# Both feed-forward projections of a two-layer decoder as block products with seven products in place of eight, on one Trainium2 core

## The chip, the core and the metric

One core of a Trainium2 chip runs the whole program in one launch. The metric is the device time of one execution in microseconds. Five engines work side by side, each through its own list of instructions in order: TensorE (PE, with its weight loads as PEld), VectorE (DVE), ScalarE (ACT), GpSimd (POOL) and SyncE (SP, which issues the DMAs). They meet only at semaphores that the kernel sets and waits for by hand.

## What is computed

The reference is one step of a hybrid decoder with two layers over 1024 prompt tokens and 8 sample tokens, all in float32: token mixer, cross attention, and the feed-forward part, which is what changes here.

```python
def conv_ffn(h, w_up_l, conv_w_l, conv_b_l, w_down_l, buf):
    u = h @ w_up_l                                   # 1032 tokens x 1024 @ 1024 x 5632
    L = u.shape[1]
    up = jnp.concatenate([buf.astype(u.dtype), u], axis=1)
    c = conv_b_l
    for j in range(CONV_W):                          # causal, depthwise, width 3
        c = c + up[:, j:j + L] * conv_w_l[j]
    a, b = jnp.split(c, 2, axis=-1)
    y = (jax.nn.silu(a) * b) @ w_down_l              # 2816 x 1024
    return y, up[:, -(CONV_W - 1):]
```

Before it h is an RMSNorm of x, and behind it x += RMSNorm(y).

## The kernel before

Everything is kept with features on the 128 partitions and the T = 1032 tokens along the free axis; `xT`, `hh`, `hl`, `Y` are tiles of 8 feature blocks by 1032 tokens. A float32 product is made of three TensorE products of the type float32r: each operand is split into a high part and the rest (`hh` and `hl` of the input, `w_hi` and `w_lo` of a weight), and `mm3` (L260) issues high by high, high by low and low by high into one PSUM bank, each with its own 128x128 weight load. ScalarE writes the high part as a copy into float32r, and a subtraction gives the low part.

Weights come as slabs of 128x1024 in an order fixed at build time (`weight_plan`, L87): SP loads one into `w_raw` (2 buffers, L230), ScalarE writes `w_hi` (3 slots, L239), GpSimd `w_lo` (L247). The plan keeps the three a few slabs ahead of TensorE.

The feed-forward part is in `stage_cross_ffn` (L1790). Its hidden features are 22 blocks j, each with two halves a and b. For a block, `up(j, 0)` and `up(j, 1)` (L2307) make the two halves of u: for each of three chunks of 344 tokens 8 feature blocks by `mm3`, so 24 matmuls into a bank, 144 for both. VectorE scales them out of PSUM into `f_u` (L2619), ScalarE starts the convolution (L2457), VectorE adds the two earlier taps (L2627 for the prompt, L2629 for the 8 samples), ScalarE applies silu (L2462), VectorE multiplies the halves (L2635), and the gate result is split in two (`f_ghi` L2473, `f_glo` L2639). `down(j)` (L2290) multiplies it at once by the rows of w_down that belong to block j: 8 output blocks by 3 chunks by 3 matmuls, 72 in all, and VectorE adds each of the 24 results into `Y` (L2654). `down(j - 1)` stands behind `up(j, 1)` on TensorE, so a block's convolution has the time of other matmuls to finish. One layer has 22 x 144 + 22 x 72 = 4752 of these matmuls, all of 344 columns.

The first block is made by `first_up` (L2192), between the last products of the cross attention's output (units of 264 columns) and the sums of squares for the norms. The last two blocks' down part, chunk by chunk, is in the class `End` (L1891 on), together with the post-norm, the residual and, after layer 0, the pre-norm of the next layer's mixer (`stage_mixer`); after layer 1 `stage_last` (L2708) does it.

## Time and profile before

| what | us |
| --- | --- |
| runs (3), median | 3277.84 (3276.75 to 3281.5) |
| profiled execution, span from its first to its last instruction | 3276.6 |
| PE busy in it | 3187.7 |
| DVE busy | 2197.5 |
| ACT busy | 1194.9 |
| POOL busy | 674.7 |
| feed-forward stretch without a pause on PE, layer 0 | 900 to 1592 |
| the same, layer 1 | 2528 to 3221 |

For the profiled execution only the span is on hand; the median of the runs lies 1.2 us above it. Matmuls overlap in their pipeline, so a matmul's own duration is longer than the distance from one start to the next; it is that distance that counts. The idle time beside a group is the engine's wait ahead of it, with what ended most of it.

### The profile page before, as it was taken

To read this page: it belongs to the slowest core of one execution; us is meant where nothing else is said; L and a number is where in the kernel's file an instruction comes from. 1 tells how busy PE (TensorE), PEld (TensorE's weight loads), DVE (VectorE), ACT (ScalarE), POOL (GpSimd) and SP (SyncE) were. 2 spreads that over 40 slices of the span, in tenths; PEclk is the share of its full clock that TensorE was granted. 3 is DMA by queue.
4 is the path that set the end of the run, shared out by engine and by line. 5 is a ranking of instruction groups with operands and counts; after the bars stand their busy time and mean duration, and the time that the engine had idled before them with its cause. 6 is when DMAs were issued, how large, how long until landed. Compare 5 with 4: busy or idle time off the path is not lost. (4 is left out here: it accounts for less than half of the span.)

```text
span 3276.6 us, 51631 instructions
## 1 busy us (share of the span) xinstructions
PE 3187.7 (97%) x21768; PEld 3034.5 (93%) x21768; DVE 2197.5 (67%) x3283; ACT 1194.9 (36%) x1904; POOL 674.7 (21%) x270
## 2 busy tenths in 40 slices
PE   8999999999999999999999999999999999999998
PEld 8999789988899999999989997899878999999997
DVE  7877764554577777777777877544545777767776
ACT  6443554344422212222445425543434122221214
POOL 1111241112321222212111113302113222122220
PEclk9999999999999999999999999999999999999999
DMA  5112342216211111111121123422152111111111
GB/s 187 47 47 66 93 147 98 78 51 232 70 46 46 47 51 40 52 46 52 51 87 41 53 65 95 173 73 78 52 225 69 52 42 51 44 52 46 46 52 60
DMA packets 80486, 245.85 MB, mean 75 GB/s; under 512 B 8064, under 2 KB 32896, under 8 KB 76672
## 3 DMA queue, kind: packets, MB, share of 16 engines
q1 hardware_dynamic: 79968, 242.50, 21.4%
q8 instruction: 172, 2.82, 0.3%
q14 instruction: 58, 0.48, 0.0%
q10 hardware_dynamic: 288, 0.06, 0.0%
HBM read 214.20 MB, written 23.04 MB: 72 GB/s over the span
## 5 line engine op out<-in xcount | busy, mean ns | idle before, releaser
L262 PE MATMUL ps<-hh,w_hi 128*128 128x344 f32 (+2 forms) x4320 | 1408.5, 326 | 30.1 <-DVE hl L1132 9.9
L264 PE MATMUL ps<-hh,w_lo 128*128 128x344 f32 (+2 forms) x4320 | 1383.0, 320 | 0.0
L263 PE MATMUL ps<-hl,w_hi 128*128 128x344 f32 (+2 forms) x4320 | 1382.8, 320 | 0.0
L247 POOL TENSOR_TENSOR w_lo<-w_raw,w_hi 128x1024 fp32r<-128x1024 f32 x266 | 674.5, 2538 | 2547.3 <-ACT w_hi L239 2547.3
L262 PEld LDWEIGHTS ps<-hh,w_hi 128*128 128x128 f32 x4320 | 815.0, 189 | 53.2 <-issue 22.2
L263 PEld LDWEIGHTS ps<-hl,w_hi 128*128 128x128 f32 x4320 | 814.9, 189 | 3.0 <-issue 0.2
L264 PEld LDWEIGHTS ps<-hh,w_lo 128*128 128x128 f32 x4320 | 814.9, 189 | 0.0
L2654 DVE TENSOR_TENSOR Y<-Y,ps 128x344 f32<-128x344 f32 x912 | 432.6, 513 | 155.7 <-PE ps L264 155.7
L239 ACT ACTIVATE w_hi<-w_raw 128x1024 fp32r<-128x1024 f32 x296 | 311.4, 1054 | 427.1 <-PE ps L264 379.9
L2457 ACT ACTIVATE f_c<-f_u,cT 128x1032 f32<-128x1032 f32 (+1 forms) x92 | 111.4, 1212 | 633.9 <-DVE f_u L2619 627.1
L263 PE MATMUL ps<-f_glo,w_hi 128*128 128x344 f32 x960 | 307.3, 320 | 0.0
L264 PE MATMUL ps<-f_ghi,w_lo 128*128 128x344 f32 x960 | 307.2, 320 | 0.0
L262 PE MATMUL ps<-f_ghi,w_hi 128*128 128x344 f32 x960 | 306.6, 319 | 0.0
L2627 DVE SCALAR_TENSOR_TENSOR f_c<-f_u,cT,f_c 128x1024 f32<-128x1024 f32 x172 | 225.2, 1309 | 98.6 <-ACT f_c L2457 95.6
L262 PEld LDWEIGHTS ps<-f_ghi,w_hi 128*128 128x128 f32 x960 | 181.1, 189 | 0.0
L264 PEld LDWEIGHTS ps<-f_ghi,w_lo 128*128 128x128 f32 x960 | 180.4, 188 | 0.0
L263 PEld LDWEIGHTS ps<-f_glo,w_hi 128*128 128x128 f32 x960 | 180.2, 188 | 0.0
L2619 DVE TENSOR_TENSOR f_u<-ps,rs 128x1032 f32<-128x1032 f32 x86 | 105.7, 1229 | 66.9 <-PE ps L264 66.7
L2629 DVE SCALAR_TENSOR_TENSOR f_c<-f_cache,cT,f_c 128x8 f32<-128x8 f32 x172 | 124.0, 721 | 6.2
L2473 ACT ACTIVATE f_ghi<-f_c 128x1032 fp32r<-128x1032 f32 x42 | 44.8, 1067 | 149.7 <-DVE f_c L2635 149.7
L1161 DVE TENSOR_TENSOR Y<-ps,rs 128x344 f32<-128x344 f32 x120 | 59.7, 508 | 47.1 <-PE ps L264 37.0
L1648 DVE TENSOR_TENSOR oq_acc<-oq_acc,oq_sq 128x384 f32<-128x384 f32 (+1 forms) x54 | 27.8, 516 | 93.3 <-ACT oq_sq L1571 91.4
(352 smaller groups left out, 3600.5 us busy)
## 6 DMA issues: line engine op xcount, KB each, us to landing
w_raw<-in_w_stream SPq DMA_DIRECT2D x296, 512.0 KB, 3.4
out_y_cols<-xT SPq DMA_DIRECT2D x6, 1376.0 KB, 8.1
xT<-out_y_cols SPq DMA_DIRECT2D x2, 4128.0 KB, 13.0
mem_keys<-in_cache_mem_k SPq DMA_DIRECT2D x6, 1024.0 KB, 5.1
Y<-in_cache_mem_k SPq DMA_DIRECT2D x6, 1024.0 KB, 7.4
mem_values<-in_cache_mem_v SPq DMA_DIRECT2D x6, 1024.0 KB, 7.9
mem_keys<-in_cache_mem_v SPq DMA_DIRECT2D x6, 1024.0 KB, 7.8
hg_set<-Y SPq DMA_DIRECT2D x32, 129.0 KB, 2.3
```

What stands on the lines that cost most here:

```text
L239: nc.scalar.activation(w_hi[:, SLOT[m], :], w_raw[:, m % RR, :], ACT.Copy).then_inc(hi_done, 1)
L247: nc.gpsimd.tensor_tensor(w_lo[:, SLOT[m], :], w_raw[:, m % RR, :], w_hi[:, SLOT[m], :].bitcast(F32), ALU.subtract).then_inc(lo_done["pool ...
L262: nc.tensor.matmul(out, whi, mhi, start=start, stop=False)
L263: nc.tensor.matmul(out, whi, mlo, start=False, stop=False)
L264: return nc.tensor.matmul(out, wlo, mhi, start=False, stop=stop)
L1161: nc.vector.tensor_tensor(dst[:, cols(c)], ps[:, u % 3, 0:CH], rs[:, cols(c)], ALU.mult)\
L2457: nc.scalar.activation(C[:, h, at], U[:, h, 2 + at.start:2 + at.stop], ACT.Identity, bias=cT[:, l, 3, col:col + 1], scale=cT[:, l, 2, col: ...
L2473: nc.scalar.activation(gh[:, j % 2, :], C[:, 1, :], ACT.Copy).then_inc(f_gh, 1)
L2619: nc.vector.tensor_tensor(tokens3(U[:, h, 2:2 + T]), ps[:, 3 * h:3 * h + 3, 0:CH], tokens3(rs[:]), ALU.mult).then_inc(f_up, 1)
L2627: dve_c(nc.vector.scalar_tensor_tensor(c[:, 0:SEQ], U[:, h, t:t + SEQ], w, c[:, 0:SEQ], ALU.mult, ALU.add))
L2629: dve_c(nc.vector.scalar_tensor_tensor(c[:, SEQ:T], ca[:, col, t, :], w, c[:, SEQ:T], ALU.mult, ALU.add))
L2654: nc.vector.tensor_tensor(y, y, b, ALU.add).then_inc(f_y, 1)
```

## The change

It treats both projections as two-by-two block products and forms each by seven products instead of eight (Winograd's form). The program of the feed-forward part is now 34 units per layer: 22 for the up-projection (a unit makes block j of both halves a and b) and 12 for the down-projection (three groups over the hidden features of 8, 8 and 6 blocks; in each 4 pairs of output blocks). Of the two-by-two split, the contracted features are cut in halves of 4 blocks (3 in the last group), the outputs are the unit's two blocks, and the tokens are cut into `cols4` quarters of 258: a pair of quarters is one two-by-two column split, and p = A or B says which pair. So a unit is 7 products x 2 pairs, each of 4 `mm3` (3 in the last group) on 258 columns: 168 matmuls (126), 5544 per layer.

What is new around them:

- The products' operands are sums and differences of blocks. For a unit's weights VectorE makes four of them, 128x512 each (`combine_block`, L2906); ScalarE writes the high part of all seven (`high_block`, L2615) and GpSimd the low part (`low_block`, L2252). Six half slots form the ring, so a block can be written when the product six blocks earlier is done.
- For the moving side there are seven operands per pair: of the normed input, once per layer, and of the gate results, at the start of each down group. VectorE makes four per pair (`combine`, L2875), and the high part is ScalarE's (14 copies); the low part is made in place, 10 by VectorE (`low`, L2897) and 4 by GpSimd (`low`, L2264).
- A product's PSUM bank stays open and later products add to it; each state is read out once. Of the 14 read-outs of a unit, VectorE adds 6 (`add_out`, L2923) and ScalarE copies 8 (`copy_out`); from unit 26 on VectorE does all 14.
- The gate result goes to DRAM (`gates`) and comes back by group in 8 loads of 4 (3) blocks by 258 columns. x is spilled to the output in DRAM and comes back at the layer's end; the result of the down part builds up in `xT`.
- The convolution adds both earlier taps of the samples in one 128x8 addition.
- The up-projection's scaling by the norm moves from PSUM to the input (`operand_of_x`).

The diff, cut to its core:

```diff
+QT = T // 4
+P_11, P_T1, P_T2, P_22, P_T3, P_21, P_T4 = range(NP)
+LANDS = [(0, 0), (1, 1), (0, 1), (0, 1), (1, 1), (0, 0), (1, 0)]
...
+def steps_of(n):
+    if n:
+        return [(n, c, p) for c in range(NP) for p in range(2)]
+    return [(0, c, p) for p in range(2) for c in range(NP - 1)] + [(0, NP - 1, p) for p in range(2)]
+def read_by(n, c):
+    return "act" if c in FIRST_TOUCH and n < FT + F_PAIRS else "dve"
...
+                def step(n, c, p):
+                        if n not in (0, *STARTS) or p == A:
+                            pe.wait_ge(f_wlo, NP * n + c + 1)
+                        if n in STARTS:
+                            low_ready(pe, STARTS.index(n), c, p)
+                        if c == P_11:
+                            if n >= 2:
+                                wait_read(pe, n - 2, P_T4, p)
...
+                            wait_read(pe, n, {P_T2: P_11, P_22: P_T1, P_T3: P_T2, P_T4: P_T3}[c], p)
...
+                        for k in range(nk):
+                            w = slice(P * k, P * k + P)
+                            last = mm3(ps[:, bank_of(n, c, p), 0:QT], block(w_hi, n, c)[:, w], block(w_lo, n, c)[:, w], high[:, k, :],
+                                       low[:, k, :], fresh and k == 0, k == nk - 1, c != P_21)
...
+                    def combine(g, c, p):
+                        if c == P_T1:
+                            x, y = plain(P_T1, p, nk), plain(P_11, p, nk)
+                        elif c == P_T2:
+                            x, y = plain(P_22, p, nk), plain(P_T1, p, nk)
+                        elif c == P_T3:
+                            x, y = plain(P_T2, p, nk), plain(P_11, p, nk)
+                        else:
+                            x, y = source_21(g, p, nk), plain(P_T2, p, nk)
...
+                        nc.vector.tensor_tensor(plain(c, p, nk), x, y, ALU.subtract).then_inc(f_t, 1)
+                    def low(g, c, p):
+                        dve.wait_ge(f_chi, hi_no(g, c, p))
+                        dve.wait_ge(f_t, t_no(g, READ_OF[c], p))
...
+                    for n in range(1, N_UNITS):
+                        if here:
+                            for p in (A, B):
+                                combine(here, P_T4, p)
+                            for c, p in ((P_T2, A), (P_T2, B), (P_T3, A), (P_21, A), (P_T4, A)):
+                                low(here, c, p)
+                        if n <= FT:
+                            conv(n - 1, 0)
+                        add_out(n, P_11, A)
+                        add_out(n, P_11, B)
+                        if n <= FT:
+                            conv(n - 1, 1)
+                            gate(n - 1)
...
+                        if n < LAST:
+                            combine_block(n + 1, P_T1)
+                        if after:
+                            for p in (A, B):
+                                combine(after, P_T1, p)
+                        add_out(n, P_22, A)
+                        add_out(n, P_22, B)
+                        if n < LAST:
+                            combine_block(n + 1, P_T2)
+                        add_out(n, P_T3, A)
+                        add_out(n, P_T3, B)
+                        if n < LAST:
+                            combine_block(n + 1, P_22)
+                        if after:
+                            for c in (P_T2, P_T3):
+                                for p in (A, B):
+                                    combine(after, c, p)
+                        add_out(n, P_21, A)
+                        add_out(n, P_21, B)
+                        if n < LAST:
+                            combine_block(n + 1, P_T3)
+                        if after:
+                            for c, p in ((P_T1, A), (P_T1, B), (P_11, A), (P_11, B), (P_22, A)):
+                                low(after, c, p)
...
-                    for j in range(1, FT):
-                        up(j, 0)
-                        up(j, 1)
-                        if j < FT - 1:
-                            down(j - 1)
+                    for n in range(1, N_UNITS):
+                        for c in range(NP):
+                            for p in (A, B):
+                                step(n, c, p)
```

VectorE's list in the middle of the feed-forward part of layer 0, one block j before (`f_u` is u, `f_c` the convolution, `Y` the down result):

```order
L2619 TENSOR_TENSOR f_u<-ps,rs 128x1032
L2622 COPY f_tail<-f_u 128x10
L2627 SCALAR_TENSOR_TENSOR f_c<-f_u,cT,f_c 128x1024
L2629 SCALAR_TENSOR_TENSOR f_c<-f_cache,cT,f_c 128x8
L2654 TENSOR_TENSOR Y<-Y,ps 128x344 x24
L2635 TENSOR_TENSOR f_c<-f_c 128x1032
L2639 TENSOR_TENSOR f_glo<-f_c,f_ghi 128x1032
```

and the same engine and place of the changed kernel, one up unit:

```order
L2952 SCALAR_TENSOR_TENSOR f_c<-f_u,cT,f_c 128x1024
L2954 TENSOR_TENSOR f_c<-f_c,f_cache 128x8
L2956 SCALAR_TENSOR_TENSOR f_c<-f_u,cT,f_c 128x1024
L2962 TENSOR_TENSOR f_c<-f_c 128x1032
L2921 TENSOR_TENSOR w_lo_f<-w_raw 128x512
L2932 TENSOR_TENSOR f_u<-f_u,ps 128x258 x2
L2921 TENSOR_TENSOR w_lo_f<-w_lo_f,w_raw 128x512
L2921 TENSOR_TENSOR w_lo_f<-w_raw,w_lo_f 128x512
```

The scaling and the 24 additions out of PSUM are gone from it; the four weight combinations (L2921) stand between six additions of 258 columns (L2932).

VectorE's list at the start of the second down group, from unit 25 into unit 26 (`hl_f` and `f_t_f` are `hl` and the tile of the last operand read as float32):

```order
L2895 TENSOR_TENSOR hl_f<-hl_f 128x4x258 x2
L2932 TENSOR_TENSOR xT<-xT,ps 128x258 x2
L2921 TENSOR_TENSOR w_lo_f<-w_lo_f,w_raw 128x512
L2895 TENSOR_TENSOR Y<-hl_f 128x4x258 x2
L2903 TENSOR_TENSOR hl<-hl_f,hh 128x4x258 x5
L2895 TENSOR_TENSOR f_t_f<-f_u,hl_f 128x4x258 x2
L2903 TENSOR_TENSOR hl<-hl_f,hh 128x4x258 x2
L2903 TENSOR_TENSOR Y_r<-Y,Y_r 128x4x258
L2903 TENSOR_TENSOR Y_r<-f_u,Y_r 128x4x258
L2903 TENSOR_TENSOR f_t<-f_t_f,f_t 128x4x258
L2932 TENSOR_TENSOR xT<-xT,ps 128x258 x6
```

Here 18 operations of 1032 columns stand in one run of the list, ahead of unit 26's first six read-outs. GpSimd's list at the same place:

```order
L2262 TENSOR_TENSOR w_lo<-w_lo_f,w_hi 128x512 x4
L2270 TENSOR_TENSOR hl<-hl_f,hh 128x4x258
L2262 TENSOR_TENSOR w_lo<-w_raw,w_hi 128x512
L2270 TENSOR_TENSOR Y_r<-Y,Y_r 128x4x258
L2270 TENSOR_TENSOR Y_r<-f_u,Y_r 128x4x258
L2270 TENSOR_TENSOR f_t<-f_t_f,f_t 128x4x258
```

Before, GpSimd had three subtractions of 128x1024 per block j; now it has seven of 128x512 per unit, and four of 1032 columns at each group's start.

## Rows read from the trace of the kernel before

**Rows 1.** The page: span and engines' busy time.

```profile
span 3276.6 us, 51631 instructions
...
PE 3187.7 (97%) x21768; PEld 3034.5 (93%) x21768; DVE 2197.5 (67%) x3283; ACT 1194.9 (36%) x1904; POOL 674.7 (21%) x270
```

**Rows 2.** Busy time by stretch: feed-forward part of layer 0, steady.

```profile
core 0: us, PE busy (x) PEld busy (x) DVE busy (x) ACT busy (x) POOL busy (x), PEclk, DMA share, GB/s
900.00:1592.00 692.00, 692.00 (x4398) 692.00 (x4397) 501.26 (x772) 156.62 (x147) 150.34 (x61) 1.00 0.14 46
```

**Rows 3.** Timeline, PE: matmuls of 256 and 264 columns; columns: start us, us.

```profile
367.11 0.28 PE L264 MATMUL ps<-mem_hi,w_lo 128*128 128x256 f32 x1
...
367.46 0.28 PE L264 MATMUL ps<-mem_hi,w_lo 128*128 128x256 f32 x1
...
829.74 0.28 PE L262 MATMUL ps<-hh,w_hi 128*128 128x264 f32 x1
...
835.91 0.29 PE L262 MATMUL ps<-hh,w_hi 128*128 128x264 f32 x1
```

**Rows 4.** Groups by shape, DVE: name, shapes, count, busy us, mean ns, idle before.

```profile
L2627 DVE SCALAR_TENSOR_TENSOR f_c<-f_u,cT,f_c 128x1024 f32<-128x1024 f32 x172 | 225.2, 1309 | 98.6 <-ACT f_c L2457 95.6
...
L2635 DVE TENSOR_TENSOR f_c<-f_c 128x1032 f32<-128x1032 f32 x42 | 51.8, 1234 | 6.5 <-DVE f_c L2629 0.5
...
L1199 DVE TENSOR_TENSOR hg_work<-hg_work,xT 128x512 f32<-128x512 f32 x20 | 13.9, 693 | 0.7
...
L653 DVE TENSOR_TENSOR mem_keys<-ps,mrs 128x256 f32<-128x256 f32 x32 | 13.4, 420 | 23.0 <-PE ps L264 22.8
```

**Rows 5.** One line, POOL's subtraction: duration ns min/median/max.

```profile
L247 POOL TENSOR_TENSOR w_lo<-w_raw,w_hi x266: 2354/2412/5464, 17.0 to 3219.8; 128x1024 fp32r<-128x1024 f32 x133
```

**Rows 6.** Additions out of PSUM, one line, DVE: duration ns min/median/max.

```profile
L2654 DVE TENSOR_TENSOR Y<-Y,ps x912: 511/514/515, 947.2 to 3199.1; 128x344 f32<-128x344 f32 x183
```

**Rows 7.** Timeline, POOL against DVE, feed-forward and before it.

```profile
1006.92 2.56 POOL L247 TENSOR_TENSOR w_lo<-w_raw,w_hi 128x1024 fp32r<-128x1024 f32 x1 [2.77 <-ACT w_hi L239]
...
1007.25 2.25 DVE L2629 SCALAR_TENSOR_TENSOR f_c<-f_cache,cT,f_c 128x8 f32<-128x8 f32 x1
...
1010.86 0.23 DVE L2629 SCALAR_TENSOR_TENSOR f_c<-f_cache,cT,f_c 128x8 f32<-128x8 f32 x1
...
834.28 12.48 POOL L247 TENSOR_TENSOR w_lo<-w_raw,w_hi 128x1024 fp32r<-128x1024 f32 x3 [1.15 <-ACT w_hi L239]
...
836.38 5.43 DVE L2541 TENSOR_TENSOR xT<-xT,Y 128x3072 f32<-128x3072 f32 x1
```

**Rows 8.** Groups by shape, ACT.

```profile
L2347 ACT ACTIVATE x_probsT<-ps 128x512 f32<-128x512 f32 x32 | 19.1, 597 | 31.2 <-PE ps L2141 31.2
```

**Rows 9.** DMA issues: KB each, median us to landing.

```profile
w_raw<-in_w_stream SPq DMA_DIRECT2D x296, 512.0 KB, 3.4
...
xT<-in_mem_cols SPq DMA_DIRECT2D x4, 512.0 KB, 5.5
```

**Rows 10.** Busy time by stretch: the first block of layer 0.

```profile
856.90:888.90 32.00, 30.88 (x173) 27.89 (x172) 11.04 (x14) 14.32 (x33) 3.68 (x2) 1.00 0.15 54
```

**Rows 11.** End of layer 0's feed-forward: first matmul of End, last evacuation read.

```profile
L1926 PE MATMUL ps<-f_ghi,w_hi x96: 314/320/626, 1592.5 to 3259.4; 128*128 128x344 f32 x96
...
1683.44 0.52 DVE L1161 TENSOR_TENSOR Y<-ps,rs 128x344 f32<-128x344 f32 x1 [3.25 <-PE ps L264]
```

**Rows 12.** The norm at a layer's end, and the last operation.

```profile
L2032 DVE TENSOR_TENSOR Y<-Y,rs 128x2752 f32<-128x2752 f32 x3 | 9.1, 3019 | 0.0
...
L2053 DVE SCALAR_TENSOR_TENSOR xT<-Y,gT,xT 128x344 f32<-128x344 f32 x24 | 12.0, 568 | 0.0
...
3271.23 1.59 DVE L2048 TENSOR_TENSOR xT<-xT,Y 128x1376 f32<-128x1376 f32 x1
```

**Rows 13.** Timeline, PE, after a pause of 2.53 us.

```profile
3227.32 0.63 PE L1926 MATMUL ps<-f_ghi,w_hi 128*128 128x344 f32 x1 [2.53 <-DVE f_glo L2688]
...
3230.72 0.32 PE L1926 MATMUL ps<-f_ghi,w_hi 128*128 128x344 f32 x1
```

1134 lines of the change are left out of this document (667 added, 467 removed).

## Prediction

> **What bounds the kernel now.** I read the page first: PE is busy for 3187.7 of 3276.6 us, DVE for 67%, ACT and POOL for 36% and 21% [rows 1]. Then the busy time by stretch: in layer 0's feed-forward part PE does not pause at all for 692 us; 4398 matmuls in 692 us are one per 0.1573 us [rows 2]. So TensorE's matmuls set the time there, and everything else hides behind them. A change that takes matmuls away can gain, as long as what it hands to DVE, POOL and ACT still hides. Last I read how DVE and POOL get on with each other, since the change loads these two.
>
> **Matmuls removed.** Before: 2 x 4752 = 9504 of 344 columns x 0.1573 = 1495 us. Now 2 x 5544 = 11088 of 258 columns. The nearest shapes are 256 columns, three starts in 0.35 us = 0.117 each, and 264 columns, 51 starts in 6.17 us = 0.121 [rows 3]. I take 0.118, since 258 is nearest to 256: 1308 us. That is **-187 us** (0.117: -198; 0.121: -153). It needs no weight load to come late: the rows at 256 columns load a 128x128 weight per matmul too and keep 0.117. For the fixed part of a matmul the Trainium skill ("TensorE: Matmul & The Clock Gate", the section "Wait — 56ns, not 53.3ns?") gives columns by 2.4 GHz plus 2.5 ns; by it the two sums would be 1386 and 1220 us and the gain 166. The trace has 14 ns over the columns' time at 344 and 10 to 11 at 256 and 264, so I keep the rows' sum.
>
> **The other engines in an up unit.** A unit gives PE 168 x 0.118 = 19.8 us. VectorE's list in it: four taps at 1.31, the product of the halves 1.23, four weight combinations like the 128x512 rows at 0.69 [rows 4], two operations on the samples at 0.23 [rows 7], six additions out of PSUM like the 256-column row at 0.42 [rows 4], 0.35 for two small copies: 12.6 us. GpSimd: seven subtractions of half the width of a row with median 2.41 [rows 5], 1.2 each, 8.4 us. Each alone fits. But they exclude each other: POOL's subtraction ran from 1006.92 to 1009.48, and DVE's 128x8 operation, 0.23 us on its own, started at 1007.25 and took 2.25, until that end. The other way round, DVE's 5.43 us from 836.38 made three POOL subtractions take 12.48 in place of 7.2 [rows 7]. The 912 additions with one operand in PSUM show no such delay: none took over 515 ns [rows 6]. The Trainium skill says it too ("GPSIMD Engine Reference", section "1. Specifications"): GpSimd's SBUF interfaces are shared with VectorE, with contention for instructions with two SBUF inputs. Without the exclusion VectorE would have 7 us to spare per unit; with it, 12.6 + 8.4 = 21.0, less about 1.9 of POOL's work that falls beside PSUM additions or a pause, plus some 20 handovers of 0.05 (an estimate; POOL's end at 1009.48 and DVE's at 1009.50 are of that size), is 20.2. T4's step needs T3's read-out with only three steps (4.2 us) between, so PE soon follows VectorE: 0.4 x 21 units x 2 layers = **+17 us** (0 if it all fits, +84 at 21.8 per unit, with nothing of POOL's beside anything).
>
> **Starts of the down groups.** At unit 22, 26 and 30 fourteen operands must be made while the old ones are still read. The order is forced: T3's operand is T2's minus 11's, and the low part of 11 overwrites 11, so the first step of the group waits for the combinations T1, T2, T3 and then the low part of 11. Time 0 is the start of the unit ahead. The gate loads (0.5 MB each, like the mem_cols rows of 5.5 us when issued in pairs) go out as steps 11 and T1 free their tiles, and the next weights behind them, 3.4 us each alone [rows 9]; I put the second half at 13. From there VectorE does four weight combinations 2.8, six combinations of 1032 columns at 1.23 = 7.4, six additions 2.5, three low parts 3.7: 16.4 us; POOL's four weight parts and one low part of 1032 (2.4) cost 7.2 more, 1.7 of it beside additions. ACT's high parts (0.6 for 512 columns [rows 8], about twice that for 1032) stay ahead of that. So the first step starts at 35 where it was due at 19.8: 15 us. Behind it, in unit 26, nine operations of 1032 and one addition (11.5) with POOL's 9.6 stand ahead of the read-out of 11 that T2's step needs, against 5.7 us of PE work: 15 more. Group 1 reaches much the same sum by another way: 7 us at T2 and 7 at T4, since VectorE first has the last block's taps and product. Group 3 has three blocks for four: 24. Sum 84 per layer, **+168 us**. Without the exclusion the same list gives 14, 15 and 11, +80 in all; the top is some 95 per layer, +190, if the gate loads land 4 us later.
>
> **Start of the feed-forward part.** Before, PE was busy for 30.88 of the 32.0 us of the first block [rows 10]. Now unit 0 waits for operands that VectorE and GpSimd make one after the other: for pair A 16 scalings, 4 combinations and the low parts, with the last norm and residual of the cross attention in the middle of VectorE's list and the weight combinations 22 and T3 behind these; for pair B all again once the last mean is known. With the prices above, step 22 A starts some 10 us late, T3 and 21 2 us each, 11 B 11 us, T1 B and T2 B some 4 each. That is 34 per layer, **+68 us** (27 per layer without the exclusion, 42 as the top: +54 to +84).
>
> **Ends of the layers.** From the first matmul of the last two blocks at 1592.5 to the ninth unit of the next mixer at 1683.4 [rows 11], 91 us hold 360 matmuls of 0.157 = 57 of real work, so 34 of sums and waits. Now 24 sums become 3 of three matmuls, but norm (3.02), residual (8 x 0.57 [rows 12]), tree and low parts of each chunk start only behind the last read-out, in a row on VectorE; my chain for the same nine units has 34 us beside the matmuls too. At the end of layer 1: read-out, squares, sum and root 4.1, six halves of 1.59 + 4 x 0.51, and the last store 3.8 (before, the last operation ended at 3272.8, 3.8 before the end [rows 12]): 30, about what sums, waits and the last chunk's norm take there now. **0 us**, between -6 and +15.
>
> **The clock.** After a pause of 2.53 us the next 12 matmuls took the 3.40 us to 3230.72, near the rate of 1.2 GHz and not of 2.4, which cost 1.5 us [rows 13]. The starts above make some ten longer pauses per layer, but half of the slow matmuls run ahead of a further wait: **+10 us** (5 to 30).
>
> **Sum.** 3276.6 - 187 + 17 + 168 + 68 + 0 + 10 = 3352.6; the median of the runs lies 1.2 above the profiled span: **3353 us**, slower.
>
> **The rivals.**
> 1. Faster. The operations of GpSimd fall into VectorE's pauses and delay nobody. Then only the chains of dependence are left: 3278 - 187 + 0 + 80 + 54 - 3 + 5 = 3227 us. For it: VectorE's list has room in the light down units. Against it: at the group starts its list is dense just where GpSimd has most to do, and every row of an overlap shows full exclusion. It decides at 93 us of loss per layer: below it the change gains.
> 2. Slower still. The up units run at 21.8, all of VectorE's and GpSimd's work in a row: 67 more, 3420 us. Against it: POOL's first subtraction of a unit waits for the weights, when VectorE waits too.
> 3. The change does not do what it says: weight loads cannot keep pace at 258 columns, say 0.140 per matmul, +244 us, about 3597. The 0.117 at 256 columns speaks against it.
>
> **How the numbers follow.** A measurement of this kernel tells 0.2% (6.5 us) from no change. Chances: the forecast 0.63 (3300 to 3400, by its own bounds), rival 1 0.17, rival 2 0.15, rival 3 0.02, within 0.2% by chance of the terms 0.03. Range: down to 3240, which takes in most of rival 1, and up to 3430 for rival 2. Faster 0.17, same 0.03, slower 0.80.
>
> **What would show it.** In the changed kernel's profile: matmuls of 258 columns starting 0.118 apart (0.14 would show rival 3); up units of 20.2 us (19.8 or 21.8 for the rivals), with subtractions of POOL stretched beyond 1.2 us and taps beyond 1.3; PE idle of about 15 us ahead of the first step of units 22, 26, 30, released by VectorE's low part, and a second wait in the same unit; some 30 us of PE idle in unit 0; GpSimd busy about 45% of the feed-forward stretch. If PE's waits there add up to less than 93 us per layer, the sign of the forecast is wrong.

## The result, and the profile after

The changed kernel takes 3350.4 us (median of 4 runs, 3348.6 to 3351.2) against 3278.2 us (4 runs, 3276.8 to 3281.5): the ratio is 1.022, 95% interval 1.0206 to 1.0235. It is slower by 72 us. The profiled execution has a span of 3349.3 us against 3276.6 before, so the two traces differ by 72.7 us, and that is what follows accounts for.

First the page of the changed kernel, to be held against [rows 1]. TensorE is busy 134 us less in a span that is 73 us longer; GpSimd is busy 1.7 times as long.

```profile
span 3349.3 us, 57862 instructions
...
PE 3053.3 (91%) x23292; PEld 2903.8 (87%) x23292; DVE 2233.6 (67%) x3027; ACT 1498.5 (45%) x2616; POOL 1177.3 (35%) x664
```

Next the busy time by stretch, layer 0's feed-forward part: unit 0 with the work around it, the steady up units, then by turns the start of a down group and the calm units behind it. The columns are: stretch (start and end in us) and its length, then busy us (and instructions) of PE, PEld, DVE, ACT and POOL, the granted clock, DMA share and GB/s.

```profile
856.00:940.00 84.00, 56.17 (x372) 53.14 (x372) 57.71 (x69) 36.48 (x64) 41.61 (x23) 0.82 0.26 88
940.00:1345.00 405.00, 405.00 (x3378) 405.00 (x3378) 316.24 (x383) 208.86 (x364) 214.23 (x140) 1.00 0.26 88
1345.00:1400.00 55.00, 33.02 (x210) 31.71 (x210) 49.65 (x45) 26.09 (x38) 31.71 (x16) 0.75 0.15 50
1400.00:1457.00 57.00, 56.02 (x467) 55.82 (x466) 14.70 (x25) 21.44 (x43) 21.27 (x17) 1.00 0.40 128
1457.00:1510.00 53.00, 27.39 (x190) 27.05 (x191) 44.84 (x41) 17.34 (x23) 30.58 (x15) 0.74 0.07 23
1510.00:1568.00 58.00, 58.00 (x485) 57.90 (x483) 23.70 (x49) 14.34 (x22) 22.65 (x18) 1.00 0.34 106
1568.00:1625.00 57.00, 37.63 (x268) 37.19 (x268) 43.49 (x60) 18.07 (x28) 29.65 (x21) 0.82 0.10 28
```

Where [rows 2] showed one stretch without a pause, there are now two kinds. In the up units and the calm down units PE never pauses, and VectorE has room (316 of 405 us). In unit 0 and at the three group starts VectorE is busy 69% to 90% of the time, PE 52% to 67%, and the granted clock falls to 0.74 to 0.82.

What the steady stretch gives: 405.00 us by 3378 matmuls is 0.1199 us each, 20.1 us per unit, with PE busy throughout. 11088 x 0.1199 = 1329 us, so the matmuls gained **166 us**.

What the rest takes back shows in PE's timeline (start, us, engine, line, operation, operands; in brackets the idle time before it and its releaser, where "issue" means that the profile shows none). These are the longest waits of unit 0 and all of group 2's start; the second of the latter is step 11 A of unit 26, which needs VectorE's low part.

```profile
881.88 0.55 PE L325 MATMUL ps<-hh,w_hi 128*128 128x258 f32 x1 [9.12 <-ACT f_u L2648]
...
907.96 0.58 PE L325 MATMUL ps<-hh,w_hi 128*128 128x258 f32 x1 [13.06 <-DVE hl L2903]
...
1458.25 0.36 PE L325 MATMUL ps<-f_t,w_hi 128*128 128x258 f32 x1 [2.22 <-DVE xT L2932]
...
1474.53 0.55 PE L325 MATMUL ps<-hh,w_hi 128*128 128x258 f32 x1 [13.15 <-issue]
...
1494.42 0.55 PE L325 MATMUL ps<-hh,w_hi 128*128 128x258 f32 x1 [11.21 <-DVE xT L2932]
```

Added up over such rows, PE's waits in layer 0 are 27.5 us in unit 0 and 21.8, 26.6 and 19.4 us at the group starts; in layer 1 they are 28.0, 21.1, 27.7 and 18.3. That is **190 us** (waits of 0.3 us and more). Beside them PE was busy longer for its matmuls in these stretches: 33.02 us for 210 of them is 7.8 more than at 0.12 each, and the other three stretches give 4.6, 5.5 and 11.5, 29 per layer, **59 us**. Some 38 us of these are matmuls at the lower clock: 212 in layer 0 and 186 in layer 1 start 0.215 apart in place of 0.1199; the rest is mostly the ends of the last matmuls ahead of waits and, in unit 0, products of another kind. The distances agree: the 5544 matmuls of a layer take 790.3 and 787.9 us from the first to the last, 249 us more than 0.1199 each. The ends of the layers gave back some 7: from the last matmul at 1656.5 to the ninth unit's read-out at 1720.7 there are 64 us, of which 30 beside matmuls (34 before), and at the end of layer 1 there are 29.8 us (32 before). In all -166 + 190 + 59 - 7 = +76, where 72.7 was measured.

VectorE's timeline says what those waits are for. This is the start of group 2: unit 25 begins at 1438.6, unit 26 is due at 1459.

```profile
1453.05 1.16 DVE L2921 TENSOR_TENSOR w_lo_f<-w_raw 128x512 f32<-128x512 f32 x1 [15.78 <-DMA w_raw<-in_w_stream]
1454.14 2.36 DVE L2895 TENSOR_TENSOR hl_f<-hl_f 128x1032 f32<-128x1032 f32 x2
...
1459.67 3.45 DVE L2895 TENSOR_TENSOR hl_f<-hl_f 128x1032 f32<-128x1032 f32 x2
1463.04 3.45 DVE L2895 TENSOR_TENSOR Y<-hl_f 128x1032 f32<-128x1032 f32 x2
...
1467.68 11.94 DVE L2903 TENSOR_TENSOR hl<-hl_f,hh 128x1032 fp32r<-128x1032 f32 x5
1479.54 2.37 DVE L2895 TENSOR_TENSOR f_t_f<-f_u,hl_f 128x1032 f32<-128x1032 f32 x2
1481.83 5.45 DVE L2903 TENSOR_TENSOR hl<-hl_f,hh 128x1032 fp32r<-128x1032 f32 x2
1487.20 3.38 DVE L2903 TENSOR_TENSOR Y_r<-Y,Y_r 128x1032 fp32r<-128x1032 f32 x1
...
1493.86 1.41 DVE L2932 TENSOR_TENSOR xT<-xT,ps 128x258 f32<-128x258 f32 x4
```

From the landing of the weights to the four additions VectorE has no pause. Step 11 A starts inside the five low parts, at 1474.53, when the third of them, its own, has just ended (1474.42); T2 A needs the first of the four additions and starts at 1494.42. The five low parts take 2.4 us each in the mean, where one takes 1.22 when nothing disturbs it. The next rows show why. First one line's durations over the whole run (ns, min/median/max), for an operation of 8 columns, the low parts of 1032, GpSimd's subtraction and the additions out of PSUM; then both timelines in a steady up unit.

```profile
L2954 DVE TENSOR_TENSOR f_c<-f_c,f_cache x88: 151/1254/1273, 933.4 to 3051.0; 128x8 f32<-128x8 f32 x88
L2903 DVE TENSOR_TENSOR hl<-hl_f,hh x54: 951/2024/3421, 864.9 to 3252.8; 128x1032 fp32r<-128x1032 f32 x40, 128x774 fp32r<-128x774 f32 x14
L2262 POOL TENSOR_TENSOR w_lo<-w_lo_f,w_hi x272: 1011/1296/2268, 869.7 to 3304.1; 128x512 fp32r<-128x512 f32 x120, 128x384 fp32r<-128x384 f32 x16
L2932 DVE TENSOR_TENSOR xT<-xT,ps x404: 406/423/426, 940.1 to 3319.5; 128x258 f32<-128x258 f32 x135
```

```profile
1005.80 1.27 DVE L2954 TENSOR_TENSOR f_c<-f_c,f_cache 128x8 f32<-128x8 f32 x1
...
1008.18 1.26 DVE L2951 COPY f_tail<-f_u 128x10 f32<-128x10 f32 x1
```

```profile
1005.09 1.95 POOL L2262 TENSOR_TENSOR w_lo<-w_lo_f,w_hi 128x512 fp32r<-128x512 f32 x1 [1.48 <-ACT w_hi L2625]
```

GpSimd's subtraction started at 1005.09 and ended at 1007.04; the operation of 8 columns, 0.15 us on its own, started at 1005.80 and ended at 1007.07. As in [rows 7], the two engines take turns by whole instructions, and an addition with one operand in PSUM (at most 426 ns in 404) is held by nobody, as in [rows 6].

### The profile page after: what moved, and what is told of

Same layout as the page of the kernel before. It is cut to its first block and busy times, and to the rows that moved or that the text cites. A ratio compares the mean times of both kernels' runs of the same rounds, so it can differ in the third digit from the quotient of the medians.

```text
span 3349.3 us, 57862 instructions
## 1 busy us (share of the span) xinstructions
PE 3053.3 (91%) x23292; PEld 2903.8 (87%) x23292; DVE 2233.6 (67%) x3027; ACT 1498.5 (45%) x2616; POOL 1177.3 (35%) x664
## 3 DMA queue, kind: packets, MB, share of 16 engines
q1 hardware_dynamic: 122752, 305.91, 27.4%
## 5 line engine op out<-in xcount | busy, mean ns | idle before, releaser
L325 PE MATMUL ps<-hh,w_hi 128*128 128x258 f32 (+3 forms) x4320 | 1352.0, 313 | 199.7 <-issue 73.2
L326 PE MATMUL ps<-hl,w_hi 128*128 128x258 f32 (+3 forms) x4320 | 1322.0, 306 | 0.0
L327 PE MATMUL ps<-hh,w_lo 128*128 128x258 f32 (+3 forms) x4320 | 1320.8, 306 | 0.0
L310 POOL TENSOR_TENSOR w_lo<-w_raw,w_hi 128x1024 fp32r<-128x1024 f32 x134 | 349.8, 2614 | 1365.0 <-ACT w_hi L302 1365.0
L2262 POOL TENSOR_TENSOR w_lo<-w_lo_f,w_hi 128x512 fp32r<-128x512 f32 (+1 forms) x272 | 380.1, 1410 | 403.6 <-DVE w_lo_f L2921 301.9
L2262 POOL TENSOR_TENSOR w_lo<-w_raw,w_hi 128x512 fp32r<-128x512 f32 (+1 forms) x204 | 319.4, 1567 | 339.3 <-ACT w_hi L2625 336.2
L325 PE MATMUL ps<-Y_r,w_hi 128*128 128x258 f32 x1056 | 301.1, 285 | 16.4 <-ACT xT L2648 14.1
L326 PE MATMUL ps<-Y_r,w_hi 128*128 128x258 f32 x1056 | 302.0, 286 | 0.0
L2932 DVE TENSOR_TENSOR xT<-xT,ps 128x258 f32<-128x258 f32 x404 | 164.8, 419 | 203.7 <-PE ps L327 203.3
L327 PE MATMUL ps<-Y_r,w_lo 128*128 128x258 f32 x1056 | 299.3, 283 | 0.0
L2921 DVE TENSOR_TENSOR w_lo_f<-w_raw 128x512 f32<-128x512 f32 (+1 forms) x136 | 141.8, 1042 | 143.6 <-DMA w_raw<-in_w_stream 121.9
L325 PEld LDWEIGHTS ps<-Y_r,w_hi 128*128 128x128 f32 x1056 | 200.9, 190 | 18.1 <-issue 14.8
L327 PEld LDWEIGHTS ps<-Y_r,w_lo 128*128 128x128 f32 x1056 | 203.3, 192 | 0.0
L326 PEld LDWEIGHTS ps<-Y_r,w_hi 128*128 128x128 f32 x1056 | 201.7, 191 | 0.0
```

The lines of the kernel that those rows point to most:

```text
L310: nc.gpsimd.tensor_tensor(w_lo[:, SLOT[m], :], w_raw[:, m % RR, :], w_hi[:, SLOT[m], :].bitcast(F32), ALU.subtract).then_inc(lo_done["pool ...
L325: nc.tensor.matmul(out, whi, mhi, start=start, stop=False, skip_group_check=reopened)
L326: nc.tensor.matmul(out, whi, mlo, start=False, stop=False, skip_group_check=reopened)
L327: return nc.tensor.matmul(out, wlo, mhi, start=False, stop=stop, skip_group_check=reopened)
L2262: nc.gpsimd.tensor_tensor(to, whole_block, block(w_hi, n, c).bitcast(F32), ALU.subtract).then_inc(f_wlo, 1)
L2921: nc.vector.tensor_tensor(block(w_lo_f, n, c), x, y, op).then_inc(f_wadd, 1)
```

## The experiments

The rows above leave two readings: the starts are long because GpSimd and VectorE hold each other out, or because of the orders and loads in them (late weights, low parts ahead of read-outs). A third question is what the slow clock adds. No run leaves out all of the operand work of the starts, so its whole price stays open.

All times are medians against runs of the kernel before on the same chip; it stayed within 3276.9 and 3278.6 us. For reading them, PE's waits in layer 0 by place, in us, added up from the timelines (waits of 0.7 us and more):

| kernel | time, us | unit 0 | group 1 | group 2 | group 3 | sum |
|---|---|---|---|---|---|---|
| the change | 3350.4 | 27.5 | 21.4 | 26.6 | 19.4 | 95 |
| e1_pool_fill | 3246.7 | 23.7 | 11.7 | 10.8 | 7.0 | 53 |
| e2_readout_first | 3326.9 | 27.4 | 21.2 | 19.5 | 12.0 | 80 |
| e3_low11_first | 3350.4 | 27.4 | 21.7 | 24.6 | 17.4 | 91 |
| e4_start_order | 3351.4 | 25.6 | 21.1 | 26.4 | 19.4 | 93 |
| e6_raw_first | 3358.5 | 27.4 | 26.4 | 26.6 | 18.4 | 99 |
| e7_hold_pool | 3331.8 | 27.7 | 24.9 | 19.9 | 14.8 | 87 |
| e9_vector_weights | 3315.5 | 26.6 | 22.1 | 18.7 | 13.1 | 81 |
| e11_late_conv | 3300.3 | 26.7 | 15.8 | 16.1 | 12.4 | 71 |
| e12_all | 3296.9 | 25.6 | 18.0 | 17.0 | 9.8 | 70 |

**e1: GpSimd writes without reading.**

```diff
-    nc.gpsimd.tensor_tensor(to, whole_block, block(w_hi, n, c).bitcast(F32), ALU.subtract).then_inc(f_wlo, 1)
+    nc.gpsimd.memset(to.bitcast(F32), 0.0).then_inc(f_wlo, 1)
...
-    nc.gpsimd.tensor_tensor(operand(c, 1, p, nk), x, operand(c, 0, p, nk).bitcast(F32), ALU.subtract)
+    nc.gpsimd.memset(operand(c, 1, p, nk).bitcast(F32), 0.0).then_inc(f_lop, 1)
```

> GpSimd's low-part subtractions of the feed-forward part (weight blocks, and its four operands of a start) write a constant instead, at the same width: the low parts of all weight blocks and of those operands are left out; VectorE, ScalarE and TensorE issue what they did. It prices how far GpSimd's two-input subtractions stretch VectorE at the starts. Theory (they hold each other out): VectorE's low parts of 1032 columns fall from 2.3-2.4 us to about 1.2, its blocks to 0.69, TensorE's waits at the starts from 190 us to about 100, and the time by 70 to 95 us, to about 3268. Rival (the starts are bound by the late raw weights and by the order of the read-outs, VectorE's own durations matter little): less than 20 us, 3330 or more. If a fill holds VectorE as a subtraction does, the durations do not fall, and the run tells nothing of the two.

Measured: 3246.7 us, 104 below the change and below the kernel before (ratio 0.9909, 0.9894 to 0.9923). VectorE's program is the same, and its lines read (same view as above, one line up in the file):

```profile
L2953 DVE TENSOR_TENSOR f_c<-f_c,f_cache x88: 152/159/167, 921.1 to 2979.9; 128x8 f32<-128x8 f32 x88
...
L2902 DVE TENSOR_TENSOR hl<-hl_f,hh x54: 951/1225/1235, 863.0 to 3157.1; 128x1032 fp32r<-128x1032 f32 x40, 128x774 fp32r<-128x774 f32 x14
...
L2950 DVE COPY f_tail<-f_u x44: 172/173/474, 919.9 to 2936.9; 128x10 f32<-128x10 f32 x44
...
1429.86 0.69 DVE L2920 TENSOR_TENSOR w_lo_f<-w_raw 128x512 f32<-128x512 f32 x1 [15.02 <-DMA w_raw<-in_w_stream]
...
1455.62 1.41 DVE L2931 TENSOR_TENSOR xT<-xT,ps 128x258 f32<-128x258 f32 x4
```

None of these operations is stretched any more: 1254 became 159 ns, 2024 became 1225. PE's waits fall by 42 us in layer 0 and 38 in layer 1, 80 in all; most of the other 24 are matmuls at a higher clock (granted 0.86 or more in each of the seven stretches). The run also takes work away from GpSimd (its blocks come after 0.53 us where they took 1.3 or more), so it prices GpSimd's subtractions as a whole: holding VectorE, and being late themselves. Its two timeline lines part the two at group 2: VectorE's row of the same 28 operations, from the first weight block to the first addition, takes 25.8 us, where it was 40.8 (1453.05 to 1493.86), and that is 15 of the 16 us that this start costs less (the distances of its steps over 0.1199 a matmul went from 31.5 to 15.4). So there nearly all of it is VectorE held out. Over both layers the six group starts cost 83 us where they cost 171, but unit 0 still costs 66 where it was 77: its price is for the most part another (e4). The Trainium skill ("GPSIMD Engine Reference", section "1. Specifications") names contention for VectorE's instructions with two SBUF inputs or in a two-port mode. The trace agrees for the first kind; the copy of 10 columns has one input and was held as well, 1.26 us, and no run shows in which mode it ran.

**e2: the read-outs ahead of the last low parts.**

```diff
-                            for c, p in ((P_T2, A), (P_T2, B), (P_T3, A), (P_21, A), (P_T4, A)):
+                            add_out(n, P_11, A)
+                            add_out(n, P_11, B)
+                            low(here, P_T2, A)
+                            add_out(n, P_T1, A)
+                            add_out(n, P_T1, B)
+                            for c, p in ((P_T2, B), (P_T3, A), (P_21, A), (P_T4, A)):
                                 low(here, c, p)
...
```

> In the first unit of each down group VectorE reads out products 11 and T1 ahead of its last low parts instead of behind them (same work, other order). Theory (TensorE stands 9 to 13 us in that unit because its banks wait behind five low parts): the 11.2, 9.1 and 5.8 us waits released by VectorE's or ScalarE's addition shrink, the low parts of T2, T3, 21 come 1 to 2 us later; in all 10 to 32 us less, about 3326. Rival (the low parts are just as late for the steps that use them, so the wait only changes its name): within 8 us of 3350.

Measured: 3326.9 us, 24 less (ratio to before 1.0151, 1.0134 to 1.0168). PE's timeline at group 2:

```profile
1458.54 0.36 PE L325 MATMUL ps<-f_t,w_hi 128*128 128x258 f32 x1 [1.81 <-DVE xT L2932]
...
1474.83 0.55 PE L325 MATMUL ps<-hh,w_hi 128*128 128x258 f32 x1 [13.16 <-issue]
...
1486.83 0.55 PE L325 MATMUL ps<-hh,w_hi 128*128 128x258 f32 x1 [4.57 <-DVE hl L2903]
```

The wait of 11.2 us became one of 4.6 us, now for the low part itself. From T4's step to T2's it is 28.3 us where it was 36.2. Group 1 did not move (21.2 against 21.4), and that stayed open until e11.

**e3: the low part that TensorE asks for first.**

```diff
-for c, p in ((P_T1, A), (P_T1, B), (P_11, A), (P_11, B), (P_22, A)):
+for c, p in ((P_11, A), (P_11, B), (P_T1, A), (P_T1, B), (P_22, A)):
```

> The low parts of product 11, which is multiplied first, are made ahead of those of T1 at the starts of the three down groups (same work, other order). Theory (TensorE stands at each start for the low part of 11, made third and fourth of a row at 2.4 us each): 13.2, 13.2 and 9.4 us waits shrink by about 4.5 each, six times, 20 to 29 us less, about 3325. Rival (the wait moves to T1, the second product): under 8 us.

Measured: 3350.4 us, no change; the rival held. PE at group 2:

```profile
1455.16 0.36 PE L325 MATMUL ps<-f_t,w_hi 128*128 128x258 f32 x1 [1.00 <-DVE xT L2932]
...
1465.91 0.56 PE L325 MATMUL ps<-hh,w_hi 128*128 128x258 f32 x1 [7.63 <-issue]
...
1491.37 0.55 PE L325 MATMUL ps<-hh,w_hi 128*128 128x258 f32 x1 [15.97 <-DVE xT L2932]
```

Step 11 A does start 5.5 us earlier behind T4's step (10.8 us, not 16.3), and T2 A starts exactly where it did: 36.2 us behind it in both kernels. The 5.5 us moved into the next wait. VectorE's row fixes the end of the stretch, and here the longest wait inside it is worth nothing by itself.

**e4: another order in unit 0.**

```diff
                     low(0, P_T2, A)
-                    normalise(4)
-                    residual(2)
                     combine_block(0, P_22)
                     combine_block(0, P_T3)
+                    normalise(4)
+                    residual(2)
```

> At the start of the feed-forward part VectorE makes the weight combinations 22 and T3 of unit 0 ahead of a normalisation and two residual steps of the output projection instead of behind them (same work, other order). Theory (TensorE's 9.1 us wait, once a layer, is for that chain): it goes, the 13.1 us wait behind it may grow by what is now done later, and the time falls by 10 to 18 us, to about 3336. Rival (the wait only moves to the B pair's operands, which stand behind the moved normalisation): within 5 us of 3350.

Measured: 3351.4 us; the rival held. The wait of 9.1 us became two of 4.3 and 2.6, and step 11 B still waits 13.1 us. In layer 1 it starts 62.2 us behind the matmul of the cross attention's output that waits 2.6 us, before and after the edit. Unit 0 ends with a row of the same kind, that of pair B, which can't start before the last mean.

**e6: raw weights ahead of the gates.**

```diff
                    for n in range(N_UNITS):
                        g = STARTS.index(n + 1) if n + 1 in STARTS else 0
-                        if g:
-                            for q in (P_11, P_T1):
...
                        if n < LAST:
                            load_raw(n + 1, 0)
                            load_raw(n + 1, 1)
...
+                        if g:
+                            for q in (P_11, P_T1):
```

> In the unit ahead of a down group the raw weights of the next unit are loaded ahead of the gates instead of behind the first four gate transfers. Theory (VectorE stands 15.8 us for raw weights and its row of combinations starts that late): the weights land some 5 us earlier, the gates some 3 us later, VectorE's row starts 2 to 4 us earlier in six starts, 12 to 24 us less, about 3332. Rival (the gates are then the last to land and the row waits for them): within 5 us of 3350.

Measured: 3358.5 us, 8 more than the change. The gates of group 2 land at 1457.6, 4.5 us behind the weights, and step 11 A of group 2 follows that of group 1 after 112.8 us, where it was 113.0: nothing gained. At group 1 a new wait came up. ScalarE's timeline, then PE's:

```profile
1341.33 1.06 ACT L2637 ACTIVATE hh<-hl_f 128x1032 fp32r<-128x1032 f32 x1 [7.91 <-DMA hl_f<-gates]
```

```profile
1345.27 0.55 PE L325 MATMUL ps<-Y_r,w_hi 128*128 128x258 f32 x1 [6.50 <-ACT xT L2648]
```

ScalarE's list has the gates' high parts ahead of a silu and two read-outs; it stood 7.9 us for the gates, and TensorE 6.5 us, at step T3 A of unit 21, for the read-outs behind. Neither theory nor rival had named that.

**e7: GpSimd holds back.** On e2:

```diff
                            if n in STARTS:
+                                pool.wait_ge(f_lo, nth(LO_ORDER, LO_LATER, STARTS.index(n), P_T2, A))
                                low(STARTS.index(n), P_T3, B)
```

> On e2_readout_first (3326.9): in the first unit of a down group GpSimd waits with its low part of T3 B until VectorE has made that of T2 A, which TensorE waits for; same work. Theory (GpSimd's subtractions hold VectorE's row out for as long as they run): 4 to 6 us of GpSimd's work leave the row ahead of T2 A, TensorE's wait there (4.6 us at the second group) shrinks by 2 to 4 us in six starts, 12 to 24 us less, about 3310. Rival (GpSimd's parts come too late for steps 21 and T4 and the wait moves there): within 5 us of 3327, or above it.

Measured: 3331.8 us, 5 above e2. The low part of T2 A came earlier (waits of 1.3 and 1.1 us where there were 4.6 and 2.6), and the same time was lost at step T3 A: 11.1 us at group 1, 4.5 and 3.6 at the others. In group 1 the total is again the same:

```profile
1345.97 0.36 PE L325 MATMUL ps<-f_t,w_hi 128*128 128x258 f32 x1 [1.71 <-DVE xT L2933]
...
1386.16 0.55 PE L325 MATMUL ps<-Y_r,w_hi 128*128 128x258 f32 x1 [11.06 <-ACT xT L2649]
```

From T4's step to T3's of the next unit it is 40.2 us, as in the change (1347.44 to 1387.66), in e2 (40.2) and in e3 (40.3). GpSimd's work, done earlier or later, costs the row the same.

**e8: what is the slow clock worth?** Products of a tile of ones fill part of the waits; beside those shown, 26 stand ahead of step 22 A of unit 0 and 38 ahead of 11 B.

```diff
+                            if n in STARTS and c == P_11:
+                                wait_read(pe, n - 2, P_T4, A)
+                                fill(bank_of(n, P_11, A), (26, 38, 26)[STARTS.index(n) - 1])
```

> On the changed kernel: ahead of the first step of the down groups (26, 38, 26) and of two steps of unit 0 (26, 38) TensorE multiplies a tile of ones by itself, 128 columns each at about 0.27 us, into a bank that the next fresh step overwrites; 7 to 10 us of each wait of 9 to 13 us are filled. Theory (about 60 us of the 73 us loss are the lower clock behind these waits, granted clock 0.75 in those stretches against 1.00): the granted clock of the stretches rises to 0.9 or more, and the time falls by 30 to 50 us, to about 3310. Rival (the low clock is not worth that much, or the chain of VectorE bounds those units at either clock): less than 10 us.

Measured: 3360.8 us, 10 more than the change. Busy time by stretch, columns as above, and PE's rows at group 1:

```profile
1345.00:1400.00 55.00, 36.59 (x246) 35.39 (x245) 51.13 (x45) 25.86 (x35) 30.02 (x15) 0.84 0.20 69
...
1457.00:1510.00 53.00, 33.19 (x256) 32.67 (x256) 45.27 (x40) 18.13 (x23) 28.71 (x13) 0.84 0.16 54
```

```profile
1351.97 0.36 PE L325 MATMUL ps<-f_t,w_hi 128*128 128x258 f32 x1 [3.80 <-DVE xT L2942]
...
1356.43 5.97 PE L2492 MATMUL ps<-ones 128*128 128x128 f32 x52
...
1392.22 0.55 PE L325 MATMUL ps<-Y_r,w_hi 128*128 128x258 f32 x1 [6.52 <-ACT xT L2658]
```

The clock rose from 0.75 and 0.74 to 0.84 in both stretches, and T4's step to T3's is 40.2 us again; in group 2 the 36.2 us from T4's step to T2's stand as before. Faster matmuls inside a stretch that VectorE bounds only wait longer. That holds for slow matmuls with a further wait of over 2 us behind them, and these are 236 of the 398. The other 162 stand behind the last such wait of their place; they are worth 15 us (an estimate, 162 by the 0.095 between the two distances), and whether a fill can get those back this run does not show: it still has 367 slow matmuls. The 10 us lost lie in unit 0 and fit a misplaced fill: the wait of 9.1 us in unit 0 lies ahead of T2 A, not of 22 A, where I put 26 products. From its first step to unit 1's, unit 0 takes 61.1 and 61.7 us in the two layers, where it took 56.4, and step 11 B comes 4.7 and 5.2 us later.

**e9: VectorE makes the low parts of the weights at the starts.** On e2; the 13 blocks made in the units around each start:

```diff
+                def on_vector(n, c):
+                    made_in = n if c == P_T4 else n - 1
+                    return made_in in STARTS[1:] or (made_in + 1 in STARTS[1:] and c != P_T4)
...
-                        nc.gpsimd.tensor_tensor(to, whole_block, block(w_hi, n, c).bitcast(F32), ALU.subtract).then_inc(f_wlo, 1)
+                        if n == 0 or not on_vector(n, c):
+                            subtract_block(pool, nc.gpsimd, n, c)
...
                             combine_block(n + 1, P_T1)
+                            low_block(n + 1, P_11)
```

> On e2_readout_first (3326.9): the low parts of the 13 weight blocks that are made in the last unit ahead of a down group and in its first unit go from GpSimd to VectorE (0.69 us each there on 512 columns, where GpSimd takes 1.28 and holds VectorE out as long); GpSimd keeps its four operand parts. Theory (the two engines share one path, and VectorE's and GpSimd's SBUF work together is what fills a start): a start loses 13 x 0.6 = 8 us of shared work, most of it on the path, and the time falls by 15 to 45 us, to about 3300. Rival (VectorE's own list is what is late, and 13 x 0.69 = 9 us more on it are worse than being held out): the time rises by 5 to 40 us.

Measured: 3315.5 us (3306.4 to 3319.0), 11 below e2, a little under the theory's range. PE at group 1:

```profile
1348.85 0.55 PE L325 MATMUL ps<-f_t,w_hi 128*128 128x258 f32 x1 [3.76 <-DVE xT L2950]
...
1386.09 0.55 PE L325 MATMUL ps<-Y_r,w_hi 128*128 128x258 f32 x1 [8.30 <-ACT xT L2660]
```

The sign is the telling part: VectorE, the engine that is late, got 13 x 0.69 = 9 us of work more per start, and the kernel is not slower but faster, because GpSimd's 13 x 1.28 are gone. T4's step to T3's fell to 37.2 us in group 1, with 8.3 of them a wait at T3 A. This is what two engines on one path do, and what a VectorE that is merely behind with its own list would not. By itself it does not part being held out from blocks that GpSimd makes late; the row of e1 does.

**e10: the same in every unit.**

```diff
-                    return made_in in STARTS[1:] or (made_in + 1 in STARTS[1:] and c != P_T4)
+                    return made_in >= 1
```

> The same, for every weight block from unit 2 on, up units too: GpSimd then does nothing in an up unit. Theory: VectorE has 12.6 + 7 x 0.69 = 17.4 us in an up unit of 20.1, still fits, and the time is that of e9 within 8 us. Rival (VectorE's row of taps of 1.28 us, gate and subtractions makes the blocks late for TensorE although the sum fits): TensorE waits in up units and the time is 20 us or more above e9.

Measured: 3424.7 us, 109 above e9; the rival held. GpSimd does nothing in an up unit, the operation of 8 columns takes 161 ns (median), and VectorE is busy 308 of the 450 us from 940 to 1390, 15.4 per unit. But PE now waits about 2 us in each up unit, most of them ahead of a T4 step, and a unit takes 22.5 us:

```profile
1081.07 0.36 PE L325 MATMUL ps<-f_t,w_hi 128*128 128x258 f32 x1 [1.96 <-DVE xT L2950]
1103.56 0.36 PE L325 MATMUL ps<-f_t,w_hi 128*128 128x258 f32 x1 [2.09 <-DVE f_u L2950]
```

```profile
1099.72 0.69 DVE L2933 TENSOR_TENSOR w_lo_f<-w_raw 128x512 f32<-128x512 f32 x1 [4.36 <-issue]
```

The low part of T4's block stands behind taps and gate in VectorE's list; the second half of the next weights is loaded only once it is made, and VectorE then stands idle 4.4 us. A sum that fits (17.4 of 20.1 in the expectation) is no proof when the list has one order and a load hangs on its last entry.

**e11: the last taps out of the way.** On e9; in unit 22 `conv(21, 0)`, `conv(21, 1)`, `gate(21)` and ScalarE's `silu(21)` go behind everything else of the unit.

```diff
-                            if n <= FT:
+                            if n < FT:
                                 silu(n - 1)
...
                             high_block(n + 1, P_21)
+                        if n == FT:
+                            silu(n - 1)
+                            load_log_exp()
```

> On e9_vector_weights (3315.5): in unit 22 the four taps, the gate and the silu of the last up unit (some 8 us of VectorE) move from the middle of the unit to its end, behind the read-outs and the row of operands; same work. Theory (TensorE's 8.3 us wait at step 21 A there is for a copy-out that ScalarE holds behind that silu): the wait goes, once a layer, and the time falls by 10 to 20 us, to about 3300. Rival (VectorE is full from the start of unit 22 for 45 us whatever the order, so the wait moves): within 5 us of 3315.

Measured: 3300.3 us (3293.4 to 3304.2), 15 below e9. PE at group 1:

```profile
1343.48 0.55 PE L325 MATMUL ps<-f_t,w_hi 128*128 128x258 f32 x1 [2.80 <-DVE xT L2951]
...
1359.04 0.55 PE L325 MATMUL ps<-hh,w_hi 128*128 128x258 f32 x1 [11.03 <-issue]
...
1389.87 0.36 PE L325 MATMUL ps<-hh,w_hi 128*128 128x258 f32 x1 [1.99 <-ACT xT L2660]
```

The 8.3 us wait, which the expectation puts at step 21 A and which lies at T3 A, is gone. That is why group 1 ignored e2, e3 and e7: some 6.5 us of taps and gate belonged to its row, and ScalarE's read-outs stood behind them.

**e12: the loads again, with the lists in step.** On e11, with the orders of e4 and e6 and:

```diff
-                            if after:
-                                for p in (A, B):
-                                    high(after, P_11, p)
...
                             high_block(n + 1, P_T2)
+                            if after:
+                                for c in (P_11, P_T1):
+                                    for p in (A, B):
+                                        high(after, c, p)
```

> On e11: also the start order of e4, and the raw weights ahead of the gates as in e6, this time with ScalarE's high parts and VectorE's combinations of the gates moved behind two weight blocks, so that no read-out stands behind a gate that has not landed; same work. Theory: e6 lost by those blocked read-outs (TensorE waits of 6.5 us that the kernel did not have), not by the loads; then VectorE's row starts 3 to 4 us earlier in six starts and e12 is 15 to 25 us below e11, about 3280, level with the kernel before. Rival (the gates, now last, bound the row): e12 within 8 us of e11 or above it.

Measured: 3296.9 us (3292.4 to 3303.3), 3 below e11, inside its spread. The 6.5 us wait of e6 does not come back, so that part of the theory held; but the gates are now what the row waits for, as the rival had it (VectorE stands 3.7 us for them at 1340.5 and 2.4 us at 1347.6).

**e13: three small things together.**

```diff
-                            for q in (P_21, P_22):
+                            for q in (P_22, P_21):
...
+                                pool.wait_ge(f_lo, nth(LO_ORDER, LO_LATER, STARTS.index(n), P_T2, A))
...
                     sum_up(5, range(KT))
+                    fill(1, 36)
...
+                                fill(bank_of(n, P_11, A), 22)
```

> On e12_all (3296.9), three orders and a fill: the gates of product 22 are loaded ahead of those of 21 (VectorE waits 2 to 2.4 us for them); GpSimd holds its part T3 B back until T2 A's low part is made, as in e7; and TensorE fills its waits ahead of step 11 B of unit 0 (36 products of a tile of ones, 0.23 us each) and ahead of the first step of each down group (22). Theory (the row of VectorE bounds the starts, and behind it TensorE runs its first 4 us at half clock): the gates' order 2 us and the held part 2 us in each of six starts, the clock 2 us in each of eight, in all 20 to 38 us less, about 3269, just below the kernel before. Rival (each moves a wait, as e3, e6, e7 and e8 did): within 8 us of 3297.

Measured: 3287.1 us (7 runs, 3283.5 to 3293.4), ratio to before 1.0029, 1.0017 to 1.0040; 10 below e12, half of the theory's low end. With the same products as the change (the fill aside), other orders and 13 blocks per start on VectorE, 63 of its 72 us are recovered, and it is still 9 us behind the kernel before. The parts of this run were not tried one by one, but the traces tell where the gain lies. Over 0.1199 a matmul, group 1 costs 19 us in either layer where it cost 25.3 and 22.6 in e12; unit 0 costs half a us more, and groups 2 and 3 together 1 and 1.5 less. At group 1 VectorE's waits for gates are 1.4 and 0.6 us (3.7 and 2.4 in e12), and from T4's step to step 11 A it is 13.8 us, not 18.3. The granted clock rose as well (0.94 from 1345 to 1400, 0.80 in e12), but from 11 A to unit 22's T4 it takes 21.2 us where it took 20.0: a gain by the fill is not to be seen.

## Why the prediction was right, and where by luck

Forecast 3353 us, measured 3350.4. By its own terms, in us:

| term | forecast | measured |
|---|---|---|
| matmuls | -187 | -166 |
| up units | +17 | 0 |
| starts of the down groups | +168 | 135 of waits, 36 of longer matmul time: +171 |
| start of the feed-forward part | +68 | 56 of waits, 23 of longer matmul time: +79 |
| ends of the layers | 0 | -7 |
| clock | +10 | in the two lines above |
| sum | +76 | +77 of the terms (rounded), +72.7 of the spans |

The mechanism held: the exclusion at the starts carries the sign. That the sum came out within 3 us is luck. The matmuls gained 21 us less than forecast and the up units cost 17 less, by reasons that have nothing to do with each other, and the start of the feed-forward part (11 more) was offset by the clock's own line and the ends. Three sums of the prediction are off by little: 21.0 - 1.9 + 1.0 is 20.1, not 20.2 (13 us for the up units, not 17), the six delays of unit 0 add up to 33, not 34, and 3352.6 + 1.2 is 3353.8.

**Matmuls.** The step "I take 0.118, since 258 is nearest to 256" was wrong. Two shapes lay at hand, 0.117 at 256 and 0.121 at 264 [rows 3], and 0.1199 was measured, nearer the far one. Both were read from short stretches; the three starts in 0.35 us of the first are good to a few thousandths at best, which times 11088 is the 21 us that were missed. By the Trainium skill ("TensorE: Matmul & The Clock Gate", section "Wait — 56ns, not 53.3ns?") a matmul of 258 columns would take 110 ns (an estimate from its columns by 2.4 GHz plus 2.5 ns). The trace has 119.9, so its figures are 109 us short after the change (1220 for 1329), and as short before (1386 for 1495): the gain of 166 that they gave is right because the two misses cancel.

**Up units.** I said 20.2 us and it is 20.1, but not for my reason. VectorE does not set the pace: PE is busy for all of 405 us, and VectorE has 316 of them, 15.7 us per unit. The exclusion is there (the 8 columns take 1.25 us where e1 has 0.16, the weight blocks straight from the raw weights 1.2 where 0.69; the taps stay at 1.27 in the median), and it costs 3.1 us per unit over my list of 12.6, or 4.3 over the 11.5 of e1; I had added nearly all of GpSimd's 8.4. Most of GpSimd's work falls into VectorE's pauses. That rival 1's mechanism holds in the up units and fails at the starts is the finer statement I should have made.

**Starts of the groups.** This term carries the sign, and it held step by step at group 2. The last raw weights landed 14.5 us after the unit ahead began (forecast 13), the first step started 36.0 us after it (forecast 35), the second wait was 11.2 us with the slower matmuls around it (forecast 15). At group 1 the second pair of waits was 4.1 and 5.8 us where I had 7 and 7, and the latter at step T3, not at T4. Without the exclusion I had 80 for this term, 54 for the next and 3227 in all; with the matmuls' miss of 21 that is 3248, and e1 measured 3246.7. That the totals meet so closely is chance in part: by place e1 costs 15.5, 15.4 and 11.6 us at the group starts of layer 0, where I had 14, 15 and 11, but 32.8 in unit 0, where I had 27. The group starts are the best support for the working, with VectorE's row, since e1 takes away what they blame, and beside it only GpSimd's own time.

**Start of the feed-forward part.** 34 per layer forecast, 28 of waits and 11 of longer matmul time measured. The 13.1 us ahead of 11 B were 11 in the forecast, the 9.1 us had been put at 22 A and lie at T2 A.

**Clock.** Forecast 10, bounds 5 to 30. There are 23 waits of over 2 us ("some ten" per layer in the forecast), and 398 matmuls start 0.215 apart, which is 38 us over 0.1199 each. The forecast put half of them ahead of a further wait, and 236 of 398 are. For those at the group starts e8 shows that faster matmuls only wait longer: they take the place of waiting that the forecast had counted in its two lines on the starts. The other 162 are 15 us, inside the bounds.

**Rivals.** Rival 1 fell: 95 us of waits per layer against its threshold of 93, and 124 with the longer matmul time. The 93 were half of a gain of 187; of the 166 that the matmuls gained, half is 83, and it is the 124 that have to be held against it. Rivals 2 and 3 are out by 20.1 us per unit and 0.1199 per matmul. GpSimd is busy 51% of the stretch from 856 to 1625, not 45%.

## What to carry to other kernels

Count the two-input SBUF work of VectorE and GpSimd as one engine's, stretch by stretch, before trading matmuls for elementwise work: here 166 us of matmuls were saved, VectorE was idle for a third of the span even so, and what decided were eight stretches of 50 to 85 us. In the six at the group starts the two engines had no room, and half of their 171 us came back in e1; unit 0 gave back 11 of 77. Where a row of one engine bounds a stretch, measure the distance between two steps at its ends (36.2 and 40.2 us here) and not the waits inside: an edit that leaves it alone has moved a wait, whatever it does to the longest one. And read what else stands in the in-order list of the engine that would wait, before a load is moved.
